# Layer norm statistics by quarters of the tokens in a two-layer streaming encoder step on one core

## The reference, cut to what matters

```python
def layer_norm(x, g, b):
    xf = x.astype(jnp.float32)
    mu = xf.mean(-1, keepdims=True)
    var = jnp.square(xf - mu).mean(-1, keepdims=True)
    return ((xf - mu) * lax.rsqrt(var + LN_EPS) * g + b).astype(x.dtype)
...
    xp = layer_norm(ALPHA * xp + y, ln1_g[l], ln1_b[l])    # norm 0: y is merge_out
    ...
    xp = layer_norm(ALPHA * xp + f, ln2_g[l], ln2_b[l])    # norm 1: f is conv_ffn
```

## Time and profile before

| | |
|---|---|
| Time of three executions | 956.98, 958.37 and 959.41 us, median 958.37 |
| Profiled execution | 956.19 us, span 954.1 us, mean granted clock 0.991 |
| TensorE busy | 927.3 us (97%) |
| VectorE busy | 607.9 us (64%) |
| ScalarE busy | 512.0 us (54%) |
| DMA | 132.93 MB, mean 139 GB/s |

### The profile page before, as it was taken

One profiled execution on the slowest core, in us unless ns is written; L12 is line 12 of the kernel. 1 busy time (PEld: TensorE's weight loads), 2 busy tenths in 40 slices (PEclk: granted clock), 3 DMA queues, 4 the chain that ended last, 5 costly groups with the idle time before them and its releaser, 6 DMA issues.

```text
span 954.1 us, 16673 instructions
## 1 busy us (share of the span) xinstructions
PE 927.3 (97%) x6442; PEld 893.9 (94%) x6442; DVE 607.9 (64%) x1287; ACT 512.0 (54%) x978; POOL 20.0 (2%) x35
## 2 busy tenths in 40 slices
PE   6999999998999999999999999999989999999996
PEld 5999989998999999999899989899989999999994
DVE  4776554578866666545587764548778666564555
ACT  3875454435855555533388554545467565553333
POOL 2000000000000000000000000000000000000000
PEclk9999999999999999999999999999999999999997
DMA  9754443544465554545835444355426554545521
GB/s 259 193 140 136 113 109 112 144 145 132 125 177 150 147 163 131 156 140 154 183 86 139 126 129 112 97 145 149 144 80 192 156 155 137 160 135 150 155 62 55
DMA packets 257767, 132.93 MB, mean 139 GB/s; under 512 B 22390, under 2 KB 254874, under 8 KB 257562
## 3 DMA queue, kind: packets, MB, share of 16 engines
q1 hardware_dynamic: 256058, 126.95, 47.9%
q0 software_dynamic: 1632, 4.93, 1.4%
HBM read 127.42 MB, written 4.57 MB: 138 GB/s over the span
## 4 chain that ended last, share of the span: by engine, by line
PE 97%; DVE 2%; DMA 1%; ACT 0%; issue 0%; SPq 0%; DVEq 0%
PE bank L622 28%; PE bank L624 28%; PE bank L623 28%; PE bank L692 3%; PE bank L840 2%; PE bank L638 1%; PE bank L644 1%; PE bank L641 1%; DVE roped_b L1405 1%; PE bank L808 1%; PE bank L795 1%; PE bank L792 1%; DMA gates<-in_x_sample 1%; PE bank L802 0%; DVE gates L1398 0%; DVE gates L1410 0%
## 5 line engine op out<-in xcount | busy, mean ns | idle before, releaser
L622 PE MATMUL bank<-act_hi,w_hi 128*128 128x320 f32 x1312 | 411.4, 314 | 0.0
L624 PE MATMUL bank<-act_hi,w_lo 128*128 128x320 f32 x1312 | 405.9, 309 | 0.0
L623 PE MATMUL bank<-act_lo,w_hi 128*128 128x320 f32 x1312 | 405.8, 309 | 0.0
L1163 DVE TENSOR_TENSOR w_lo<-raw,w_hi 128x1024 fp32r<-128x1024 f32 (+1 forms) x236 | 284.2, 1204 | 113.6 <-ACT w_hi L916 112.5
L916 ACT CAST w_hi<-raw 128x1024 fp32r<-128x1024 f32 (+1 forms) x236 | 243.4, 1032 | 154.7 <-PE bank L624 147.4
L622 PEld LDWEIGHTS bank<-act_hi,w_hi 128*128 128x128 f32 x1312 | 246.6, 188 | 3.9 <-issue 2.2
L623 PEld LDWEIGHTS bank<-act_lo,w_hi 128*128 128x128 f32 x1312 | 246.6, 188 | 0.2
L624 PEld LDWEIGHTS bank<-act_hi,w_lo 128*128 128x128 f32 x1312 | 246.4, 188 | 0.0
L622 PE MATMUL bank<-h_hi,w_hi 128*128 128x320 f32 x352 | 109.5, 311 | 0.0
L624 PE MATMUL bank<-h_hi,w_lo 128*128 128x320 f32 x352 | 108.9, 309 | 0.0
L623 PE MATMUL bank<-h_lo,w_hi 128*128 128x320 f32 x352 | 108.9, 309 | 0.0
(11 more groups left out here) (195 smaller groups left out, 976.4 us busy)
## 6 DMA issues: line engine op xcount, KB each, us to landing
raw<-in_w_in SPq DMA_DIRECT2D x62, 512.0 KB, 3.8
raw<-in_w_gate SPq DMA_DIRECT2D x44, 512.0 KB, 3.8
raw<-in_w_up SPq DMA_DIRECT2D x44, 512.0 KB, 4.3
raw<-in_w_down SPq DMA_DIRECT2D x32, 448.0 KB, 3.7
raw<-in_w_o SPq DMA_DIRECT2D x16, 512.0 KB, 4.0
raw<-in_w_down SPq DMA_DIRECT2D x16, 512.0 KB, 4.0
raw<-in_w_in SPq DMA_DIRECT2D x16, 256.0 KB, 5.0
raw<-in_w_pa SPq DMA_DIRECT2D x32, 128.0 KB, 2.8
```

The source lines that it names most:

```text
L622: pe.matmul(out, wh, hi[:, k0 + c, :], start=begin and c == 0, stop=False)
L623: pe.matmul(out, wh, lo[:, k0 + c, :], start=False, stop=False)
L624: mm = pe.matmul(out, wl, hi[:, k0 + c, :], start=False, stop=end and c == n_chunks - 1)
L1163: ve.tensor_tensor(w_lo[:, slot, :, :].rearrange("p c e -> p (c e)")[:, 0:w], raw[:, slot, 0:w], hi.bitcast(F32), ALU.subtract).then_inc(l ...
```

## The change

The mean and mean square are still summed on TensorE, but for the variance the 320 tokens are cut in four parts of 80. For each part a matmul with 32 columns of `mean_w` writes to its own 32 partitions, so that a bank holds all 320 tokens in 80 columns. Square, subtraction, root and reciprocal work on 128 x 80. Four matmuls (`spread_rstd`), each with one column of the identity repeated 128 times as weights, bring 1/std of each part back to all partitions, in a bank of units' results that is free at this time. VectorE scales from that bank. The mean itself is still made on all 320 columns, now by the last matmul of the step and copied by ScalarE after the root. VectorE takes the reciprocal ahead of the first two subtractions of the mean. Of the key copies on ScalarE, one stands ahead of the affines instead of three.

```diff
@@ the uses of a norm, and their banks @@
-            while len(USES) % 4 != 3:
+            while len(USES) % 4 != 0:
...
-                                   "values": ("o",), "norm": ("mean", "square")}.get(_s, (_s,))]
+                                   "values": ("o",), "norm": ("mean", "part", "square")}.get(_s, (_s,))]
@@ TensorE @@
+        def rstd_bank(i):
+            return bank[(TILE[("gate", 1)] + 1) % 4 if i == 0 else 3]
...
                 if kind == "params":
+                    if l > 0:
+                        spread_rstd(l - 1, 1)
...
-                    for t in KEY_TILES:
+                    for k, t in enumerate(KEY_TILES):
+                        if k == 3:
+                            spread_rstd(l, 0)
                         step(l, "kv", t)
...
+                        for g in range(4):
+                            mm = pe.matmul(out[32 * g:32 * (g + 1), 0:PART], mean_w[:, 0:32],
+                                           src[:, g * PART:(g + 1) * PART], start=start, stop=not start)
...
                     pe.matmul(mean, mean_w, sum_q, start=True, stop=False)
-                    pe.matmul(square, mean_w, sum_sq, start=True, stop=False)
+                    by_part(part, sum_q, True)
+                    by_part(square, sum_sq, True)
                     pe.wait_ge(r_ready, n(l, KC * i + KC, 2 * KC))
+                    by_part(part, gates[:, KC - 1, :], False).then_inc(mean_parted, 1)
+                    pe.wait_ge(squared, n(l, KC * i + KC, 2 * KC))
+                    by_part(square, gates[:, 2 * KC - 1, :], False).then_inc(square_parted, 1)
                     done(pe.matmul(mean, mean_w, gates[:, KC - 1, :], start=False, stop=True))
-                    pe.wait_ge(squared, n(l, KC * i + KC, 2 * KC))
-                    done(pe.matmul(square, mean_w, gates[:, 2 * KC - 1, :], start=False, stop=True))
+                    if l == DEPTH - 1 and i == 1:
+                        spread_rstd(l, i)
...
+            def spread_rstd(l, i):
+                pe.wait_ge(rstd_ready, n(l, i + 1, 2))
+                out = rstd_bank(i)
+                for g in range(4):
+                    mm = pe.matmul(out[:, g * PART:(g + 1) * PART], id32[:, 32 * g:32 * g + 1].to_broadcast([P, P]),
+                                   part_rstd, start=True, stop=True)
+                mm.then_inc(rstd_spread, 1)
@@ ScalarE @@
+                    act.wait_ge(mean_parted, n(l, i + 1, 2))
+                    sc.activation(part_sq, part[:, 0:PART], ACT.Square).then_inc(mean_squared, 1)
+                    act.wait_ge(var_ready, n(l, i + 1, 2) + 2)
+                    sc.activation(part_spread, part_spread, ACT.Sqrt, bias=eps_t[:]).then_inc(spread_ready, 1)
                     b, v = spare(l, ("mean", i))
                     act.wait_ge(spare_done, v)
-                    sc.activation(mean_sq, b[:, 0:TOK], ACT.Square).then_inc(mean_squared, 1)
                     sc.copy(mean_q, b[:, 0:TOK]).then_inc(mean_copied, 1)
-                    act.wait_ge(var_ready, n(l, i + 1, 2) + 2)
-                    sc.activation(spread, spread, ACT.Sqrt, bias=eps_t[:]).then_inc(spread_ready, 1)
...
-                        for t in KEY_TILES[0:3]:
-                            keys_out(l, t)
+                        keys_out(l, KEY_TILES[0])
                         split_tiles()
-                        for t in KEY_TILES[3:]:
+                        for t in KEY_TILES[1:]:
                             keys_out(l, t)
@@ VectorE @@
-                    ve.tensor_tensor(spread, b[:, 0:TOK], mean_sq, ALU.subtract).then_inc(var_ready, 1)
+                    ve.tensor_tensor(part_spread, square[:, 0:PART], part_sq, ALU.subtract).then_inc(var_ready, 1)
...
+                    dve.wait_ge(spread_ready, n(l, i + 1, 2))
+                    ve.reciprocal(part_rstd, part_spread).then_inc(rstd_ready, 1)
...
-                    dve.wait_ge(spread_ready, n(l, i + 1, 2))
-                    link(ve.reciprocal(rstd[:], spread))
+                    dve.wait_ge(rstd_spread, n(l, i + 1, 2))
```

More of the change, by code:

```diff
@@ L42 @@
 EPS = 1e-5
+PART = (256 + 64) // 4
 NEG = -1e30
@@ L194 @@
 USE = {u: n for n, u in enumerate(USES) if u}
-USED = {u: n + 1 for n, u in enumerate(USE)}
+USED = {u: n + 1 for n, u in enumerate(u for u in USE if u[0] not in ("part", "square"))}
 N_USES = len(USED)
@@ L326, in build @@
         shift, sum_q, sum_sq, mean_q, mean_sq, spread = [vectors[:, k, :] for k in range(6)]
-        rstd = roped_b
+        part_sq, part_rstd = mean_sq[:, 0:PART], roped_b[:, 0:PART]
+        part_spread = spread[:, 0:PART]
         eps_t, warm = sb("eps_t", [P, 1]), sb("warm", [P, 1])
@@ L407, in released @@
                     "o": (o_split, n(l, i + 1, PAIRS) + 1), "shift": (shift_ready, n(l, i + 1, 2)),
-                    "mean": (mean_copied, n(l, i + 1, 2)), "square": (var_ready, n(l, i + 1, 2) + 2)}[kind]
+                    "mean": (mean_copied, n(l, i + 1, 2)), "part": (mean_squared, n(l, i + 1, 2)),
+                    "square": (var_ready, n(l, i + 1, 2) + 2)}[kind]
         def tile_released(l, tile):
@@ L603, in claim @@
                     pe.wait_ge(*released(l, USES[back]))
-                elif at < 3:
-                    pe.wait_ge(var_ready, n(l, 2, 2))
+                elif l > 0:
+                    last = len(USES) - 4 + at
+                    while USES[last] is None:
+                        last -= 4
+                    pe.wait_ge(*released(l - 1, USES[last]))
+                else:
+                    pe.wait_ge(var_ready, 2)
                 return bank[4 + at % 4]
@@ L762, in step, with by_part @@
                     settled()
-                    square = claim(l, ("square", i))[:, 0:TOK]
+                    part = claim(l, ("part", i))
+                    settled()
+                    square = claim(l, ("square", i))
+                    def by_part(out, src, start):
+                        for g in range(4):
+                            mm = pe.matmul(out[32 * g:32 * (g + 1), 0:PART], mean_w[:, 0:32],
+                                           src[:, g * PART:(g + 1) * PART], start=start, stop=not start)
+                        return mm
                     pe.matmul(mean, mean_w, sum_q, start=True, stop=False)
-                    pe.matmul(square, mean_w, sum_sq, start=True, stop=False)
+                    by_part(part, sum_q, True)
+                    by_part(square, sum_sq, True)
                     pe.wait_ge(r_ready, n(l, KC * i + KC, 2 * KC))
+                    by_part(part, gates[:, KC - 1, :], False).then_inc(mean_parted, 1)
+                    pe.wait_ge(squared, n(l, KC * i + KC, 2 * KC))
+                    by_part(square, gates[:, 2 * KC - 1, :], False).then_inc(square_parted, 1)
                     done(pe.matmul(mean, mean_w, gates[:, KC - 1, :], start=False, stop=True))
-                    pe.wait_ge(squared, n(l, KC * i + KC, 2 * KC))
-                    done(pe.matmul(square, mean_w, gates[:, 2 * KC - 1, :], start=False, stop=True))
+                    if l == DEPTH - 1 and i == 1:
+                        spread_rstd(l, i)
                 elif kind == "tails":
@@ L1056, in step @@
                 elif kind == "norm":
+                    part = bank[4 + USE[("part", i)] % 4]
+                    act.wait_ge(mean_parted, n(l, i + 1, 2))
+                    sc.activation(part_sq, part[:, 0:PART], ACT.Square).then_inc(mean_squared, 1)
+                    act.wait_ge(var_ready, n(l, i + 1, 2) + 2)
+                    sc.activation(part_spread, part_spread, ACT.Sqrt, bias=eps_t[:]).then_inc(spread_ready, 1)
                     b, v = spare(l, ("mean", i))
                     act.wait_ge(spare_done, v)
[L1059 removed]
                     sc.copy(mean_q, b[:, 0:TOK]).then_inc(mean_copied, 1)
[L1061 to L1062 removed]
                     g0, b0 = (P_LN1G, P_LN1B) if i == 0 else (P_LN2G, P_LN2B)
@@ L1392, in step @@
                     dve.wait_ge(mean_squared, n(l, i + 1, 2))
-                    b, v = spare(l, ("square", i))
-                    dve.wait_ge(spare_done, v)
-                    ve.tensor_tensor(spread, b[:, 0:TOK], mean_sq, ALU.subtract).then_inc(var_ready, 1)
+                    dve.wait_ge(square_parted, n(l, i + 1, 2))
+                    square = bank[4 + USE[("square", i)] % 4]
+                    ve.tensor_tensor(part_spread, square[:, 0:PART], part_sq, ALU.subtract).then_inc(var_ready, 1)
+                    rstd = rstd_bank(i)[:, 0:TOK]
                     def centre(o):
                         ve.tensor_tensor(gates[:, o, :], gates[:, o, :], mean_q, ALU.subtract).then_inc(centred, 1)
+                    dve.wait_ge(spread_ready, n(l, i + 1, 2))
+                    ve.reciprocal(part_rstd, part_spread).then_inc(rstd_ready, 1)
                     dve.wait_ge(mean_copied, n(l, i + 1, 2))
```

4 lines of the change are left out of this document (3 added, 1 removed).

## The result

| | before | changed |
|---|---|---|
| Median of four timed executions | 957.89 us | 949.10 us |
| Their range | 956.98 to 959.41 | 948.34 to 950.65 |
| Profiled execution | 956.19, span 954.1 | 949.25, span 947.2 |

The ratio is 0.9911 with a 95% interval of 0.9891 to 0.9931: the change makes the kernel 0.9% faster, clear of the 0.3% that can be told from nothing. A second comparison, with other executions of both kernels, gave 949.33 us against 956.84 (0.9914, 0.9895 to 0.9934). The forecast was 953.0 with a range of 949.9 to 956.4.

A forecast was written before the change was run, and what follows sets the result against it. The prediction took the four layer norms' latency chain over three engines as the bound. From 956.19 profiled, minus 4.1 (chain) and 1.3 (clock), came 950.8; with 2.18 up to the median, 953.0 us, range 949.9 to 956.4.

The forecast's parts named there:

- What bounds the kernel: Four layer norms: a latency chain over three engines, 5.81 us to the first scaling in each, not any engine's busy share.
- Sets of narrow matmuls, 0.16 us each: Statistics on TensorE: four 32-row matmuls of 80 columns overlap, so a set costs 0.16 us.
- the change to narrow tiles: Statistics on TensorE: switching between full and narrow tiles costs 0.10 us of 0.19, the rest hidden.
- Subtraction, root and reciprocal: Norm chain on VectorE and ScalarE: at 80 columns these steps take 0.24, 0.37 and 0.66 us.
- The wait that takes over: Norms 0: spreading 1/std queues on TensorE behind six transposes; the reciprocal is ready 0.5 us before it may start.
- Sum of the chain: Earlier first scalings in the four norms: 0.97 + 0.97 + 0.7 + 1.48 = 4.1 us.
- the slower rival: Statistics: four 32-wide tiles do not overlap, 0.54 us a set, each norm loses 0.3 us, 959.6 us; chance 0.06.
- The clock: Groups behind norms: less TensorE idle makes 1.2 GHz stretches rarer, gaining 0 to 2.6 us; one stretch, 1.3, taken.
- The key copies, costed at nothing: Behind ScalarE's affines: four key copies instead of two cost nothing, as TensorE's group ends later; uncovered, some 0.8 us.
- Earlier by d: After the norm: a first scaling that is earlier by d moves the rest of the kernel by d.
- Carrying the profiled execution to the median: Whole kernel: the median stands 2.18 us above the profiled execution, so 950.8 becomes 953.0.
- both low stretches gone: Rival on TensorE's clock: both stretches at the lower clock vanish, 951.7 us; chance 0.23.

The follow-up runs named there:

- the wide reciprocal: The changed kernel with its reciprocal made on 128x320 instead of 128x80; median 954.57 us, against 955.99 for the kernel before.
- the moved spreading: The changed kernel with the spreading of 1/std put ahead of transposes it stood behind on TensorE; median 947.37 us against 949.33 for the changed kernel.
- The filled kernel: The kernel before with unused 256-column matmuls in TensorE's idle around three norms, chain as before; median 953.5 us against 956.84.
- the short reciprocal: The kernel before with its reciprocal on 80 of 320 columns, all else as before; median 950.54 us against 955.99.
- the three sets: Three sets of timed experiments, each with executions of the kernel before beside it, at 956.84, 955.99 and 955.22 us.

## Why the prediction was wrong, point by point

- **What bounds the kernel.** Right. The gain lies in the norms alone; outside them only the 0.2 us of the first input moved, and that is chance (its arrival varies by 1.6 us between profiles of before).
- **Sets of narrow matmuls, 0.16 us each.** Right (0.15), and the change to narrow tiles cost 0.09 where 0.10 was taken. The row of two 64-wide tiles carried over to four.
- **Subtraction, root and reciprocal.** 0.24, 0.37 and 0.66 were taken, 0.23, 0.36 and 0.65 measured. Lines through two shapes of the same instruction, or of its like, were good to 0.01 us.
- **The wait that takes over.** Right: the spreading stood behind the transposes that wait for the copied mean. In norms 0 the reciprocal ended 0.5 us before the spreading began, as forecast. With the queue gone the first scaling came 0.35 us sooner in norms 0 and 0.8 in norm 1 of layer 0, as the wide reciprocal and the moved spreading both show.
- **Sum of the chain.** 4.1 us forecast, 4.8 measured (1.2, 0.75, 1.2, 1.65 against 0.97, 0.7, 0.97, 1.48). The mechanism was right, and the size came out a sixth larger: the first scaling came 4.60 us after the start in norms 0 (4.7 to 4.9 was to show the forecast right), 5.07 in norm 1 of layer 0 and 4.25 in the last. In norms 0 the sixth transpose was done 0.12 us sooner than summed, and the spreading with its way out took 1.05 us instead of 1.17. By its own terms the last norm comes to 4.39 us and a gain of 1.42, not to 4.33 and 1.48 (the sum stays 4.1), and the slower rival with a tile change in each pass to about 975, not 973.
- **The clock.** The step that failed first, "I take one, 1.3": both stretches went, for 1.34 + 0.57 us in the profiled executions. The price was off too: the stretch at the layer's turn was to cost "about the same" 1.3, and 0.7 of it was given back to the wait for the next weights. The filled kernel gains the same 2.0 us with the old chain, so before's idle was the cause of the two stretches. How much idle the clock bears is not shown: the short reciprocal, with less idle than before, has half clock behind norm 0 of layer 0, where before had none.
- **The key copies, costed at nothing.** Moving two of them behind the affines was not nothing in the other direction: the short reciprocal alone loses 0.8 us in each norm 0 to them. "Earlier by d" carried over to the group only because the change moves them; the text did not name this wait as what would be late next.
- **Carrying the profiled execution to the median.** The step that failed most: "the median shown is 2.18 above the profiled execution, so 953.0". The runs show in its place that the changed kernel's median (949.10) stands 0.15 below its profiled execution (949.25). The 2.18 us belong to before. The clocks of its first executions are not on record, but their 956.98 to 959.41 us lie where the larger sets have almost only those at 0.989 and 0.986, and the changed kernel has none of these. This is 2.3 of the 3.9 us that the forecast missed; the chain is 0.7, the clock 0.6 and the start 0.2. The first four executions of before were also high: 957.89 against 956.84, 955.99 and 955.22 in the three sets; the 2.18 was in part the luck of three executions.
- **The range.** Its lower end took the best chain and both stretches, but kept the 2.18 us on top, and so missed by 0.8. The rival "both low stretches gone" had the condition right, and its 951.7 is off by the same 2.3 us and the longer chain gain.

## What to carry to other kernels

A value that is alike on all partitions can be cut over the partitions when an instruction is priced by its columns, if bringing it back is cheap and the narrow matmuls lie side by side; check in the trace of any narrow matmul that they do. When a change takes idle time from TensorE, count the clock as a possible gain of its own, and look at the granted clock of each timed execution before a difference between profiled and timed ones is carried over to the new kernel. After shortening a chain, ask of each in-order queue on it what stands ahead of the next step: here two key copies on ScalarE (0.8 us) and the transposes ahead of the spreading on TensorE (0.35 to 0.8 us) stood against a gain of 1.2 us in a norm.

## What the runs showed of the hardware that was not expected

- Unused matmuls of 256 columns (five in each norm 0, five at the layer's turn) raised the granted clock in the groups from 0.84 and 0.86 to 1.00 and made the kernel faster (953.5 against 956.84 us).
- The clock can fall behind a norm with less idle ahead of it and stay up behind one with more: 0.84 with 1.30 + 0.95 us of idle (short reciprocal, norm 0 of layer 0), 1.00 with 1.30 + 1.66 (the same place in five profiles of before).
- Four 32-wide tiles in fp32 run a set of four 80-column matmuls in 0.15 us. By columns alone the set would take 0.54, which is 3.6 times as much; with full-width tiles it took 0.87, 5.8 times, since there each pass took 0.109 us instead of the 0.067 of its 80 columns. The Trainium skill, "TensorEngine Tiling (Array Packing)", Theoretical Speedup, gives up to 4 times for 32 columns: the traces agree by columns, and show more against the real full-width set. Its drain on a change of mode (Key Properties) fits the gap of 0.09 us ahead of the first narrow matmul; no run tests that by itself.
- VectorE scales from a bank at 0.479 us a tile, no slower than from on-chip memory (0.487 before).
